# An RWKV recurrence's core woven into dense rows: one step for each level of the triangular inverse

## The reference, cut to what matters

```python
def step(state, inp):
    r_t, w_t, k_t, v_t, a_t, b_t = inp
    sa = jnp.einsum('bhvk,bhk->bhv', state, a_t)
    state = state * w_t[:, :, None, :] + sa[..., None] * b_t[:, :, None, :] + v_t[..., None] * k_t[:, :, None, :]
    return state, jnp.einsum('bhvk,bhk->bhv', state, r_t)
```

## Time and profile before

| | us |
|---|---|
| median of 3 runs | 1943.49 (1943.46 to 1946.0) |
| the profiled execution | 1944.14 |
| its span | 1942.0 |
| TensorE busy | 1912.8 |
| VectorE busy | 983.5 |
| ScalarE busy | 777.3 |
| GpSimd busy | 291.6 |

### The profile page before, as it was taken

How to read it: one execution, slowest core, us unless ns; L and a number is a source line. 1 busy time by engine, 2 the same in 40 slices (tenths; PEclk the granted TensorE clock), 3 DMA queues, 4 the chain that set the end, 5 groups by cost and what they waited for, 6 DMA issues and landing times.

```text
span 1942.0 us, 27868 instructions
## 1 busy us (share of the span) xinstructions
PE 1912.8 (98%) x11648; PEld 1566.1 (81%) x11648; DVE 983.5 (51%) x1550; ACT 777.3 (40%) x1260; POOL 291.6 (15%) x286
## 2 busy tenths in 40 slices
PE   8999999999999999999999999999999999999997
PEld 6877777778888888888788888888888888888886
DVE  6666666656432333367745344459444432333365
ACT  6665233254443332345433333354233433232345
POOL 2001323302210010122000000015110311010124
PEclk9999999999999999999999999999999999999999
DMA  5222111145233323233322222222322342223221
GB/s 201 66 87 76 62 51 56 62 140 172 95 106 122 111 89 103 91 109 125 114 66 70 72 81 82 87 76 87 108 95 81 112 137 98 98 98 98 97 87 55
DMA packets 60080, 185.71 MB, mean 96 GB/s; under 512 B 6595, under 2 KB 11843, under 8 KB 59828
## 3 DMA queue, kind: packets, MB, share of 16 engines
q1 hardware_dynamic: 59956, 183.94, 28.5%
HBM read 173.69 MB, written 10.22 MB: 95 GB/s over the span
## 4 chain that ended last, share of the span: by engine, by line
PE 88%; DVE 5%; ACT 2%; issue 2%; POOL 1%; DMA 1%; SPq 0%; DVEq 0%; POOLq 0%; ACTq 0%
PE P L578 26%; PE P L580 25%; PE P L579 25%; DVE AREN L1771 2%; DVE AREN L1774 1%; POOL AREN L2516 1%; ACT WHI L1177 1%; PE P L1109 1%; DVE WLO L1778 1%; PE P L914 1%; PE P L926 1%; PE P L930 1%; PE P L767 0%; POOL AREN L2519 0%; PE P L1060 0%
## 5 line engine op out<-in xcount | busy, mean ns | idle before, releaser
L578 PE MATMUL P<-HH,WHI 128*128 128x512 f32 x1528 | 613.1, 401 | 6.2 <-DVE HL L1791 3.6
L580 PE MATMUL P<-HH,WLO 128*128 128x512 f32 x1528 | 596.3, 390 | 0.0
L579 PE MATMUL P<-HL,WHI 128*128 128x512 f32 x1528 | 595.6, 390 | 0.0
L1177 ACT ACTIVATE WHI<-RAW 128x1024 fp32r<-128x1024 f32 x302 | 318.0, 1053 | 419.6 <-PE P L580 418.8
L1778 DVE TENSOR_TENSOR WLO<-RAW,WHI 128x1024 fp32r<-128x1024 f32 x302 | 375.9, 1245 | 144.7 <-ACT WHI L1177 143.2
L578 PE MATMUL P<-ARR,WHI 128*128 128x512 f32 (+1 forms) x920 | 353.1, 384 | 0.0
L579 PE MATMUL P<-ARR,WHI 128*128 128x512 f32 (+1 forms) x920 | 352.9, 384 | 0.0
L580 PE MATMUL P<-ARR,WLO 128*128 128x512 f32 (+1 forms) x920 | 352.8, 384 | 0.0
L578 PEld LDWEIGHTS P<-HH,WHI 128*128 128x128 f32 x1528 | 286.8, 188 | 76.3 <-issue 6.7
L580 PEld LDWEIGHTS P<-HH,WLO 128*128 128x128 f32 x1528 | 286.8, 188 | 61.5
L579 PEld LDWEIGHTS P<-HL,WHI 128*128 128x128 f32 x1528 | 287.2, 188 | 56.3 <-issue 1.0
(11 more groups left out here) (313 smaller groups left out, 1424.5 us busy)
## 6 DMA issues: line engine op xcount, KB each, us to landing
RAW<-in_w_in_dram SPq DMA_DIRECT2D x117, 512.0 KB, 3.3
RAW<-in_w_ff_dram SPq DMA_DIRECT2D x64, 512.0 KB, 3.3
RAW<-in_w_ml_dram SPq DMA_DIRECT2D x64, 512.0 KB, 3.3
RAW<-in_w_out_dram SPq DMA_DIRECT2D x16, 512.0 KB, 3.3
RAW<-in_w_pg_dram SPq DMA_DIRECT2D x16, 512.0 KB, 3.3
AREN<-in_xT_dram SPq DMA_DIRECT2D x16, 256.0 KB, 5.7
s_gates<-AREN SPq DMA_DIRECT2D x16, 256.0 KB, 2.0
RAW<-in_w_ab_dram SPq DMA_DIRECT2D x8, 512.0 KB, 3.3
```

The costliest lines, as they stand in the source:

```text
L578: e.matmul(out, hi, H[0][:, s], start=first, stop=False)
L579: e.matmul(out, hi, H[1][:, s], start=False, stop=False)
L580: return e.matmul(out, lo, H[0][:, s], start=False, stop=last)
L1177: e.activation(WHI[n % NSPL][:, :], RAW[n % NRAW][:, :], ACT.Copy).then_inc(*D.act.sig("whi", n))
```

## The change

- The two steps `la` and `lb` of a level become one step `V`. It keeps Y (the masked product, in the old X buffer) and S (in the old Q buffer), and computes both S'Y and Y'S in one step: 16 matmuls per pair. VectorE masks one with the level's mask, now with the diagonal in it, and copies the other. A step `V6` finishes Q (a sum with the identity) and holds the two products that stood beside the last level. A factor 0.5 is applied by ScalarE in W. GpSimd's preparation is two additions of the identity.
- T's matmuls follow G's in the same step and go to banks 6 and 7, shared by the pairs: the products of h go to bank 6 + h. VectorE still masks them in step T, which comes after G's masks. The mean of the round before, at `la` 2 before, stands in step T and waits for those masks; variance, root and the rest move one or two steps on.
- N's matmuls go to M's step, with the bank 6 or 7; the state's first step stays in N, the second goes from S to O.
- Steps stand at distances by weights (20 to 28), 51 steps over the same 125 rows.
- In the front, only kk is in the first step; the maximum, ka and kp are in the second. The steps stand at V3, V6, M and N.
- The loads of x leave `gates_in` and stand in rows 30, 34, ... 58 of the merge.

```diff
-        out += [("G", q, 0), ("T", q, 0)]
-        for lev in range(1, 6):
-            out += [("la", q, lev), ("lb", q, lev)]
-        out += [("W", q, 0), ("M", q, 0), ("N", q, 0)] + ([("S", q, 0)] if q < 3 else []) + [("O", q, 0)]
-    return out + [("E", 3, i) for i in range(3)]
+        out += [("G", q, 0, 27), ("T", q, 0, 25)]
+        out += [("V", q, lev, (22, 22, 26, 28, 24, 25)[lev - 1]) for lev in range(1, 7)]
+        out += [("W", q, 0, 25), ("M", q, 0, 25), ("N", q, 0, 22), ("O", q, 0, 25)]
+    return out + [("E", 3, i, 20) for i in range(3)]
...
+    steps, r = core_steps(), 0
+    n = sum(s[3] for s in steps)
+    for what, q, lev, rows in steps:
+        group = ["c", "e"] + (["f"] if q < 3 and (what in "MN" or (what, lev) in (("V", 3), ("V", 6))) else [])
+        put_steps(at, A_GA + r * 125 // n, group)
+        r += rows
...
 TensorE
                 def mean(q, b):
-                    o = take(b, C.act.at("y", q))
+                    o = take(b, C.act.at("y", q), CO[0].dve.at("t", min(q + 1, 3), 1))
...
+                    if what == "T" and q:
+                        mean(q - 1, bw)
...
+                        o = [v3(take(6 + h)[:, 128 * jj:128 * jj + 128], 2) for h in range(2)]
+                        for j, p in jp4:
+                            for h in range(2):
+                                d = e.matmul(o[h][rws[p], j, :], AR[rws[h], j, 0, p, :], BK[rws[h], j, 3 * p, :],
+                                             start=True, stop=True)
+                        d.then_inc(*C.pe.sig("t", q))
+                        if jj == 1:
+                            free[6] = free[7] = C.dve.at("t", q, 1)
+                    if what == "V" and lev < 6:
+                        marks = (C.dve.at("Y", q, 0), C.pool.at("S0", q)) if lev == 1 else (C.dve.at("S", q, lev - 1),)
+                        o = [v3(take(b, *marks)[:, 0:256], 2) for b in (b0, b1)]
+                        for i in range(2):
+                            for j, p, h in jhp:
+                                at, to = rws[p ^ (h & (lev - 1))], rws[p ^ (h & lev)]
+                                a, x = v3(Qm, 4)[at, 2 * j + h, :], v3(Xm, 4)[at, 2 * j + h, :]
+                                d = e.matmul(o[h][to, j, 64 * i:64 * i + 64], *((a, x), (x, a))[i], start=True, stop=True)
+                        d.then_inc(*C.pe.sig("v", q, lev))
+                        free[b0] = free[b1] = C.dve.at("S", q, lev)
...
 VectorE
+                    if what == "V" and lev < 6:
+                        w.wait_ge(C.pe.at("v", q, lev))
+                        mul(hj(Xm), both(b0, 128, 128)[:, :, :, 0:64], lb4(lev)).then_inc(*C.dve.sig("Y", q, lev))
+                        e.tensor_copy(hj(Qm), both(b0, 128, 64)).then_inc(*C.dve.sig("S", q, lev))
+                    if what == "V" and lev == 6:
+                        w.wait_ge(C.pe.at("x1", q))
+                        add(v3(Qm, 4), v3(o0[:, 0:256], 4), i64b).then_inc(*C.dve.sig("Q", q))
...
 SyncE, merge
+                    if i % 4 == 2 and 30 <= i < 62:
+                        x = (i - 30) // 4
+                        load(f"x{x}", 1, ar(XB + x), A["xT"][:, T * x:T * (x + 1)])
...
-                load(f"x{j}", 1, ar(XB + j), A["xT"][:, T * j:T * (j + 1)])
```

More of the change, by code:

```diff
@@ L847, in second @@
                 def second(what, q, lev):
-                    if what == "la":
+                    if what == "T" and q:
+                        mean(q - 1, bw)
+                    if what == "V":
                         if lev == 1:
-                            o = take(bw, *[cc(8 + 2 * jj + j) for j in range(2)])
+                            o = take(bw, CO[0].dve.at("t", q, 1), *[cc(8 + 2 * jj + j) for j in range(2)])
                             for j in range(2):
@@ L884, in second @@
                         free[b1] = C.act.at("y", q)
-                for what, q, lev in core_steps():
+                for what, q, lev, _ in core_steps():
                     _, _, Vq, _, _, _ = p_.q(q)
@@ L911, in core @@
[L911 to L921, removed]
-                            for j in range(2):
[L924 to L948, removed]
@@ new lines, in core @@
+                    if what == "V" and lev == 6:
+                        o = [take(b, C.dve.at("S", q, 5), C.act.at("vt", q, 1)) for b in (b0, b1)]
+                        xo = (o[1][:, 0:128], o[0][:, 256:384])
+                        for h in range(2):
+                            for j in range(2):
+                                for p in range(2):
+                                    e.matmul(tx(o[0][:, 0:256], j, p, h), tx(Xm, j, p, h), tx(Qm, j, p, h), start=True,
+                                             stop=True)
+                                for p in range(2):
+                                    d = e.matmul(xo[h][rws[p ^ h], 64 * j:64 * j + 64], Gu(rws[1 - p], j, p, h, 0),
+                                                 VU[rws[1 - p], j, p, 64 * h:64 * h + 64], start=True, stop=True)
+                        d.then_inc(*C.pe.sig("x1", q))
+                        free[b0], free[b1] = C.act.at("x1", q, 1), C.act.at("x1", q, 0)
@@ L969, in core @@
                             free[(b0, b1)[p]] = C.dve.at("QT", q, p)
[L970 to L971 removed]
+                        o = take(bw, C.act.at("U", q, 1))
                         for j, p, h in jhp:
@@ L1557, in second @@
                 def second(what, q, lev):
-                    if what == "la" and lev == 1:
+                    if what == "V" and lev == 1:
                         w.wait_ge(C.pe.at("av", q), C.pe.at("w", q - 1))
@@ L2217, in front @@
                     mul(v2["kk"], Kq, col("k_k")).then_inc(*F.dve.sig("kk", q))
+                    yield
+                    w.wait_ge(F.pe.at("ss", q))
+                    e.tensor_scalar(tmp, bank(6 + jj)[:, 0:256], 1e-24, None, op0=ALU.max).then_inc(
+                        *F.dve.sig("max", q))
                     w.wait_ge(F.pool.at("rk", q - 1))
@@ L2274, in second @@
                     Vq = p_.q(q)[2]
-                    if what == "la":
-                        if lev == 2 and q:
-                            centred(q - 1, ow)
+                    if what == "T" and q:
+                        centred(q - 1, ow)
+                    if what == "V":
                         if lev == 3:
@@ L2280, in second @@
                             mul(v2[f"bon{q % 2}"], v3(ow[:, 0:256], 2), Vq).then_inc(*C.dve.sig("bon", q))
-                        if lev == 5 and q:
+                        if lev == 4 and q:
                             result(q - 1, ow)
-                    if what == "lb" and lev < 5:
-                        add(Qm, Qm, o0[:, 128:384]).then_inc(*C.dve.sig("Q", q, lev))
-                    if what == "N":
-                        state(2 * q, o1)
-                for what, q, lev in core_steps():
+                for what, q, lev, _ in core_steps():
                     if wide:
@@ L2320, in core @@
                             add(p_.QTD[:, :, p, :], AR[:, :, 1, p, :], xj[:, 1]).then_inc(*C.dve.sig("QT", q, p))
-                    if what == "S":
+                    if what == "N":
+                        state(2 * q, o1)
+                    if what == "O" and q < 3:
                         state(2 * q + 1, o0)
```

95 lines of the change are left out of this document (33 added, 62 removed).

## The result

The changed kernel takes 1919.03 us (median of 4 runs, 1918.39 to 1919.65); the kernel before, on the same chip, 1943.73 us. The ratio is 0.987, 95% interval 0.9858 to 0.9883: 24.7 us faster, where 21.7 had been forecast (1922, range 1916 to 1931). The profiled execution took 1919.65 us with a span of 1917.9, against 1944.14 and 1942.0 before, so 24.1 us of span.

A forecast was written before the change was run, and what follows sets the result against it. TensorE, busy for 98% of the span, was taken to bound the kernel by what it issues. 16.6 + 1.8 + 6.4 - 4.1 - 0.7 + 1.8 = 21.8 us off 1944.14 gave 1922.3, stated as 1922, range 1916 to 1931.

The forecast's parts named there:

- (1) Levels: Core's levels in the gates' projection: la and lb steps give way to V steps of 1.41 us; 16.6 us saved.
- The 60 cycles of the Trainium skill: V steps: some 60 cycles of overhead per matmul, 25 ns, 1.95 us a step; the sum would shrink to some 11 us.
- (2) Fewer rows: Between dense rows: T joins G's step, S joins O, the mean stands alone for three rounds; 1.8 us saved.
- (3) Old waits: Gates' projection: TensorE's waits at L914 (3.6), L939 (2.0) and L962 (0.8) go, 6.4 us; L897's 0.8 stays.
- (4) New waits: Step T and levels: the mean waits 4.1 us for VectorE's masks, plus 0.7 allowed in the levels; bounds 2 and 12.
- hidden: GpSimd ahead of V1: it loses three of five operations and V1 stands two rows behind T, so no wait.
- The front's step one on: The front's products max, ka, kp move one step on, into V6; VectorE stays under two thirds busy: costs nothing.
- (5) Reload: Merge: without x's loads between the gates' loads the weight tile lands sooner; 1.8 of a 2.0 us wait saved.
- B: Levels: V steps cost the lb price, 1.75 us each, so 16.6 becomes 9.8 and the time 1929; chance 0.13.
- C: Levels: VectorE's chain of masked product and copy replaces the old waits, 20 levels late by 0.4 us: 1930; chance 0.17.
- D: Levels: the strided copy makes VectorE pace every V step, from a copy of about 1.6 us on; slower; chance 0.04.
- E: Merge and joined rows: the reload and row merging do nothing, only the levels' arithmetic counts: 1926; chance 0.06.

The follow-up runs named there:

- two_corners: The changed kernel with the V steps' products on the partitions of p alone, so only two of four 64x64 corners are used: 1937.0 us.
- corner_twice: The changed kernel with the V steps' matmuls reordered, j innermost, each corner used twice in turn with shares still a quarter each: 1921.89 us.
- front_order: The changed kernel with the front's order of before (kk, ka, kp in the first step, the maximum alone in the second): 1924.26 us.
- copy_twice: The changed kernel with VectorE's copy in every V step made twice, the second behind the first by a wait: 1929.29 us.
- reload_alone: The kernel before with only the loads of x moved, from between the gates' loads to rows 30 to 58 of the merge: 1942.25 us against 1944.07.
- no_reload: The changed kernel with the loads of x put back between the gates' loads: 1921.29 us.
- t_late: The changed kernel with VectorE masking both pairs before adding the identity in step T, and T one or two rows later: 1916.92 us.

## Why the prediction was right, by its steps

The mechanism and the time came out as forecast; the gain was 3 us larger, 24.7 for 21.7, within the forecast's own range. That the total came so near is in part luck: the levels gave more than forecast, the joined rows and the clock took nearly as much back. The table goes through TensorE's timeline of the stretch in both kernels: each step's cost from dense matmul to dense matmul as in the prediction (less 0.23, plus 0.11), less the waits of the list, added up by kind.

| us, steps of all four rounds | before | after | saved | forecast |
|---|---|---|---|---|
| levels (without the mean) | 72.5 | 51.5 | 21.0 | 16.6 |
| G and T | 13.8 | 12.8 | 1.0 | 1.4 |
| the mean, rounds 0 to 2, now in a row of its own | 2.5 | 3.1 | -0.6 | -0.6 |
| S and O | 11.9 | 10.9 | 1.0 | 1.0 |
| M and N | 15.2 | 17.0 | -1.9 | 0 |
| listed waits | 7.2 | 5.5 | 1.7 | 1.6 |
| half the clock behind the mean of round 0 | 0 | 1.7 | -1.7 | 0 |

These are 20.5 of the 20.9 us between the landmarks. With 0.8 ahead of the core and 2.5 behind it the sum comes to the measured 24.

- *(1) Levels.* Forecast 16.6, with 1.41 us for a V step. Measured 1.30 in the lone steps; by the same count of steps 51.8 - 7.0 - 26.0 = 18.8. I had taken `la`'s row for the rate and then gone 10% above it for fear of the even levels' order; the rate is 14.9 ns. The cause that I named, the same corner twice in turn, was the lesser one: the share of the fullest corner sets the rate (two_corners), the order adds 15% (corner_twice). The banks, which I had named as well, were not tried alone. The other 2 us of the table's 21.0 are time lost inside the old steps that the list of waits doesn't name: beyond its listed waits the last `lb` took 2.1, 2.0 and 2.0 us in rounds 1 to 3, and V6, with the same matmuls, takes 1.75.
- *The 60 cycles of the Trainium skill.* By the Trainium skill, TensorEngine Tiling (Array Packing), section Instruction Overhead, the estimate was 25 ns a matmul instruction and a sum of some 11 us. The trace shows 14.9 ns over four corners; what the same page of the Trainium skill states under Key Properties, that tiles execute in parallel, fits the trace better, and its figure is below what one corner needed here, 59 ns.
- *(2) Fewer rows.* The mis-sized term: forecast 1.8, and -0.5 in the table. S joining O gave its 1.0, and the mean by itself cost its 0.6. G with T's matmuls takes 238.03 - 234.73 - 0.23 + 0.11 = 3.18 us in the kernel after. Before, by the dense matmuls around G and around T in round 1,

```profile
242.37 0.40 PE L580 MATMUL P<-HH,WLO 128*128 128x512 f32 x1
...
244.68 0.50 PE L578 MATMUL P<-HH,WHI 128*128 128x512 f32 x1
...
245.94 0.39 PE L580 MATMUL P<-HH,WLO 128*128 128x512 f32 x1
...
246.93 0.50 PE L578 MATMUL P<-HH,WHI 128*128 128x512 f32 x1
```

it was 2.31 - 0.12 = 2.19 and 0.99 - 0.12 = 0.87, so 3.06. T's joining G brings 0.1 us of loss in rounds 1 and 2, not 0.35 of gain: TensorE now goes from 64x128 matmuls to 64x64, back and again for the second pair. At each change of form the next start is 0.12 to 0.17 us later than the rate gives (58 ns for the 32 of G in the earlier trace rows, 17 for those of T): 236.15 - 235.06 for 16 of G, 236.54 - 236.15 for 16 of T. The Trainium skill, TensorEngine Tiling (Array Packing), section Key Properties, says that a change of the tiling mode drains TensorE; whether it is a drain or not, no run here shows. The gain of 1.0 in the table comes from rounds 0 and 3, where the old T stood one row behind G and cost 1.60 and 1.43 instead of 0.87. Its last matmuls started when VectorE's masks of G were done, a wait inside a group that the list doesn't show. Before, in round 3:

```profile
353.46 2.48 DVE L1771 TENSOR_TENSOR AREN<-P,CST 128x512 f32<-128x512 f32 x4 [4.84 <-PE P L897]
...
355.15 0.70 PE L907 MATMUL P<-AREN 64*64 64x64 f32 x24
356.00 0.45 PE L907 MATMUL P<-AREN 64*64 64x64 f32 x8
```

N's move into M's step, which I had at nothing, cost 1.9. M took 1.87 and N's own matmuls 1.14 in round 1 before, 3.01 together; now they take 3.34, and 0.3 to 0.6 more than before in each round. Here, too, each pair goes from 64x64 matmuls (L946, L950) to 128x64 ones (L956), so the form (the tile's shape) changes three times where it had not within M. In either step, putting the first form's matmuls of both pairs ahead of the second form's would save two of the three changes. It was not tried, so that the change of form is the cause is argued, not shown.
- *(3) Old waits.* Forecast 6.4; all 7.2 of the list went, L897's 0.8 included, and so did the 0.4 ahead of L799 that I had not counted. I had argued that the front's backlog has the same work in any order. front_order brings both back, L897's at 0.4 and L799's in full.
- *(4) New waits.* Forecast for the mean 2.1, 1.2 and 0.8; measured 2.13, 1.28 and 1.11. The chain through VectorE's order was right in the place (behind the gate row's evacuation) and in the size. What the first of them does to the clock, 1.7 us in the profiled execution, I had at nothing. Missed: 0.7 at V1 of round 0 for GpSimd, whose four additions start behind the front's products and take 0.96 us each (193.51 to 197.34); "hidden" held for rounds 1 to 3. The 0.7 us allowed in V4 to V6 did not come, but by a margin of tenths (copy_twice).
- *The front's step one on: nothing.* Wrong in kind. In the place it had before it costs 5.2 us in this kernel. I had looked at what waits for these products, and not at what stands behind them in VectorE's queue.
- *(5) Reload.* Forecast 1.8; measured 1.65 in reload_alone and 1.99 in no_reload.

Rivals B, C and D (V at 1.75, VectorE pacing the levels, slower than before) are refuted; C and D's mechanism is real and starts with less than one more copy of 0.41 us per level, where D had put it at a copy of 1.6 us. Of E one half was right: the joined rows gave nothing (-0.5), the reload gave its share. The dense rows are interrupted 50 times and not 51, for T of round 0 has no matmul of its own.

## What to carry to other kernels

Where an engine that is nearly always busy has small work woven into its queue, count what each step costs at its edges, take for its rate the fullest corner of the array and not the number of matmuls, and count the changes of matmul form inside a step, too. Behind a wait of 2 us look at the granted clock before you price the wait. A wait inside a group of matmuls may stand in no list; it shows when like steps cost unlike times. A wait is made by the queue of the engine that releases it: write down what stands ahead of the releasing instruction in *its* order, an evacuation that waits for the dense row's end above all, and place the step before it or two rows behind. An instruction moved within such a queue is priced by what stands behind it where it lands and where it leaves, even if nobody waits for it.

## What the runs showed of the hardware

- Float32 matmuls of 64x64: 14.9 ns from start to start over four corners in even shares, 17.1 with each corner twice in turn, 22 with 3/8 of them in one corner, 29.5 in two corners.
- Where 64x128 and 64x64 matmuls alternate inside a step, the start behind each change is 0.12 to 0.17 us late.
- Behind waits of 2.0 to 2.1 us TensorE's granted clock fell to 0.50 for 3.4 us in three profiled executions (the changed kernel, two_corners, t_late), which cost 1.7 us in the first; behind the same wait of 2.13 us it stayed at 1.00 in five others.
- A copy from PSUM of 128x256 float32 takes 0.41 us on VectorE and 0.33 from start to start, like a product with a constant.
